# Moving the decays of the second pair of old states behind the first two additions on VectorE

## The reference, cut to what matters

```
new_state[b, head] = exp(sum of dA over the 16 tokens) * old_state[b, head]      (the decay)
                   + sum over tokens of B[token] * dt*decay*x[token]              (the addition)
y_off[token]       = C[token] . old_state * exp(cumulated dA)                      (uses the old state, undecayed)
```

## Time and profile before

| what | us |
|---|---|
| median of 3 runs (lowest, highest) | 1969.38 (1961.38, 1970.03) |
| time of the profiled execution | 1973.41 |
| its span (first to last instruction) | 1971.8 |
| TensorE busy | 1912.7 (97%) |
| VectorE busy | 1059.2 (54%) |
| ScalarE busy | 739.8 (38%) |
| GpSimd busy | 112.4 (6%) |
| mean granted clock of TensorE | 0.977 |

### The profile page before, as it was taken

One profiled execution on the slowest core, in us unless ns is written; L12 is line 12 of the kernel. 1 busy time (PEld: TensorE's weight loads), 2 busy tenths in 40 slices (PEclk: granted clock), 3 DMA queues, 4 the chain that ended last, 5 costly groups with the idle time before them and its releaser, 6 DMA issues.

```text
span 1971.8 us, 31921 instructions
## 1 busy us (share of the span) xinstructions
PE 1912.7 (97%) x12877; PEld 1858.7 (94%) x12877; DVE 1059.2 (54%) x1339; ACT 739.8 (38%) x1157; POOL 112.4 (6%) x219
## 2 busy tenths in 40 slices
PE   8999999999799999999999999998799999999998
PEld 7999999999799999989998998987799999999998
DVE  6442443345687664556567677765745433442444
ACT  5221332223477643334545445542333221221222
POOL 2000000000012100001011011100000000000000
PEclk9999999999899999999999999997899999999999
DMA  4222222222222243334224323322622222222222
GB/s 141 74 66 75 73 78 73 76 69 79 101 73 70 66 127 89 96 92 122 85 71 114 105 84 108 98 71 76 220 74 70 75 75 74 74 76 74 75 66 77
DMA packets 268066, 171.68 MB, mean 87 GB/s; under 512 B 6534, under 2 KB 259642, under 8 KB 267677
## 3 DMA queue, kind: packets, MB, share of 16 engines
q1 hardware_dynamic: 239840, 129.52, 22.8%
q0 software_dynamic: 7072, 26.34, 4.2%
q10 hardware_dynamic: 21072, 14.69, 2.4%
HBM read 150.03 MB, written 20.48 MB: 86 GB/s over the span
## 4 chain that ended last, share of the span: by engine, by line
PE 88%; DVE 6%; ACT 3%; issue 2%; DMA 1%; DVEq 0%; ACTq 0%
PE pu L633 79%; PE pn L890 2%; PE pn L830 1%; PE pn L840 1%; PE pn L858 1%; PE pn L881 1%; ACT w_hi L987 1%; PE pn L862 1%; DMA merged<-gate_spill 1%; DVE w_lo L1376 1%; PE pu L901 0%; DVE xc L1370 0%; PE pu L692 0%; PE pn L650 0%; DVE bc L1370 0%
## 5 line engine op out<-in xcount | busy, mean ns | idle before, releaser
L1376 DVE TENSOR_TENSOR w_lo<-w_raw,w_hi 128x1024 fp32r<-128x1024 f32 x240 | 295.7, 1232 | 504.0 <-ACT w_hi L987 502.0
L633 PE MATMUL pu<-act_hi,w_hi 128*128 128x320 f32 x2336 | 543.2, 314 | 19.0 <-DVE h_b L1829 9.0
L633 PE MATMUL pu<-act_lo,w_hi 128*128 128x320 f32 x2336 | 535.4, 310 | 2.0 <-DVE act_lo L1417 1.9
L633 PE MATMUL pu<-act_hi,w_lo 128*128 128x320 f32 x2336 | 535.2, 310 | 0.0
L987 ACT ACTIVATE w_hi<-w_raw 128x1024 fp32r<-128x1024 f32 x240 | 253.6, 1056 | 540.0 <-PE pu L633 536.3
L633 PEld LDWEIGHTS pu<-act_hi,w_hi 128*128 128x128 f32 x2336 | 394.0, 189 | 33.0 <-issue 26.0
L633 PEld LDWEIGHTS pu<-act_lo,w_hi 128*128 128x128 f32 x2336 | 393.0, 189 | 3.3 <-DVE act_lo L1417 3.0
L633 PEld LDWEIGHTS pu<-act_hi,w_lo 128*128 128x128 f32 x2336 | 393.3, 189 | 0.0
L633 PE MATMUL pu<-h_hi,w_hi 128*128 128x320 f32 x1056 | 241.4, 310 | 0.7 <-DVE ff_g L1434 0.7
L633 PE MATMUL pu<-h_lo,w_hi 128*128 128x320 f32 x1056 | 241.4, 309 | 0.0
L633 PE MATMUL pu<-h_hi,w_lo 128*128 128x320 f32 x1056 | 241.4, 309 | 0.0
(11 more groups left out here) (319 smaller groups left out, 2011.7 us busy)
## 6 DMA issues: line engine op xcount, KB each, us to landing
w_raw<-in_ffn_w_up_dram SPq DMA_DIRECT2D x87, 512.0 KB, 3.8
w_raw<-in_w_in_dram SPq DMA_DIRECT2D x73, 512.0 KB, 3.9
w_raw<-in_ffn_w_down_dram SPq DMA_DIRECT2D x32, 512.0 KB, 3.8
w_raw<-in_w_br_ssd_dram SPq DMA_DIRECT2D x16, 512.0 KB, 3.4
w_raw<-in_ffn_w_down_dram SPq DMA_DIRECT2D x16, 384.0 KB, 3.3
es<-e_spill POOLq DMA_DIRECT2D x40, 128.0 KB, 2.9
merged<-gate_spill POOLq DMA_DIRECT2D x8, 640.0 KB, 4.9
h_a<-in_state_ssd_h_dram POOLq DMA_DIRECT2D x8, 512.0 KB, 6.2
```

The costliest lines, as they stand in the source:

```text
L633: ins = pe.matmul(dst[:, h, :], w[:, side, c, :], a[:, k, h * HALF:(h + 1) * HALF], start=(at == 0), stop=(at == n - 1))
L1376: dve.tensor_tensor(w_lo[:, side, :, :], w_raw[:, side, :, :], w_hi[:, side, :, :].bitcast(F32), ALU.subtract).then_inc(s["w_lo_done"], 1)
```

## The change

Two lines change places, in each of the two branches. With a middle unit (groups 0 to 2), `decay_states(1)` moves from ahead of `xbc_taps` to behind `new_states(0)`, ahead of `xbc_silu`. Without one (group 3), `new_states(0)` goes ahead of `decay_states(1)`. The instructions, their number and their sizes stay as they are, and so do the programs of the other engines.

```diff
                 if middle:
                     for q in range(PAIRS):
                         add_square(SQ_GRP + g * SQG + q, q % 2, SEQ)
-                    decay_states(1)
                     xbc_taps(*middle[0][1:])
                     new_states(0)
+                    decay_states(1)
                     xbc_silu(*middle[0][1:])
                 else:
+                    new_states(0)
                     decay_states(1)
-                    new_states(0)
                     for q in range(PAIRS):
                         add_square(SQ_GRP + g * SQG + q, q % 2, SEQ)
```

## The result

The changed kernel took 1980.66 us (median of 6 runs, 1978.08 to 1985.12) beside 1969.51 for the kernel before (6 runs, 1961.38 to 1972.05): a ratio of 1.0069, with a 95% interval of 1.0047 to 1.0091. That is 9 to 18 us slower, with 13.6 us in the middle; the plain difference of the two medians is 11.15 us. Forecast were 1981.8 us and +12.4. The profiled execution took 1982.1 us with a span of 1980.5, 8.7 more than the span before; its mean clock is 0.977, as before.

What follows compares the result with a forecast made beforehand. TensorE, busy 1912.7 of 1971.8 us, was taken to bound the kernel. Delay of 9.1 us plus 3.3 us of clock gave +12.4 us on the median 1969.38: 1981.8 us (0.63% slower), range 1971.5 to 1990.

Steps and rivals of the forecast that it cites:

- The old place was free: Ahead of VectorE's weight cut: removing the decays brings the first additions no earlier, 0 us, bound 0.1 us a group.
- The new place has no cover: Behind the first pair's additions VectorE has no idle time: 2.28 us delay in each of 4 groups, 9.1 us.
- The size of the waits: TensorE's waits for the additions to the second pair of states: 18.1 us in sum in place of 9.0.
- the two terms of the forecast: Whole kernel: 9.1 us of delay plus 3.3 us for TensorE's clock, 12.4 us in all.
- The clock term: TensorE's units behind the pauses: 1.64 us each in groups 0 and 1, nothing more in 2 and 3; 3.3 us.
- rival 2: Group 3's low clock ahead of its pause falls elsewhere; 9.0 us come back, 1972.8 us (+0.2%); chance 0.13.
- Delay alone: All four groups: only the delay counts, clock about 0; +9.1 us, 1978.5 us (0.46%); chance 0.24.
- every resumption pays the full 2.65 us: TensorE's units behind all four pauses lose clock in full: +15.4 us, 1984.8 us (0.78%); chance 0.12.
- Absorption later: Later TensorE waits (weight tile, merge DMA) take up part of the delay: 1979.5 us, or 1977.2; chance 0.09.

Runs made afterwards that it cites:

- second comparison: The unaltered changed kernel measured again, on another chip's set of runs, against the kernel before: 1.0059 (1.0036 to 1.0082), +11.6 us, median 1981.84.
- fifth experiment: Changed kernel plus 16 additional matmuls on TensorE behind each group's last product, against the kernel before: 1.0048 (1.0030 to 1.0066), +9.4 us, median 1979.9.
- first four experiments: Decays moved in groups 0 to 2 only, in group 3 only; decays shortened in changed order, in old order; against the kernel before: 1.0031, 1.0018, 1.0023, 0.9997.
- groups 0 to 2 alone: Changed kernel with group 3 back in its old order, against the kernel before: 1.0031 (1.0020 to 1.0042), +6.1 us, median 1977.05.
- group 3 alone: Kernel before with the decays moved in group 3 only, against the kernel before: 1.0018 (1.0002 to 1.0035), +3.5 us, median 1974.4.
- changed order, short decays: Changed kernel with the second pair's decays done for one of 8 streams only, against the kernel before: 1.0023 (1.0011 to 1.0035), +4.5 us.
- old order, short decays: Kernel before with the second pair's decays done for one of 8 streams only, against the kernel before: 0.9997 (0.9983 to 1.0010), -0.6 us.
- changed order with early additions: Changed kernel with the second pair's additions directly behind its decays, against the kernel before: 1.0011 (0.9997 to 1.0024), +2.2 us, median 1972.07.

## Why the prediction was right

**The old place was free: shown.** The forecast of 0 gained ahead of the additions held to the hundredth for the convolution (2.74 us behind the start of ScalarE's weight half in both), and shortening the decays there by 7.5 us changed the time by -0.6 us, with an interval from -3.3 to +2.0. The weight cut came early by 0.28 us, where about 0.3 was forecast.

**The new place has no cover: shown.** TensorE restarts 6.95 us behind the second addition to the first pair in group 0 (858.71 - 851.76), where 6.96 was forecast. With the decays 1.87 us shorter at the new place most of the loss went; with the additions placed early in both orders, the decays' place was again worth 10.0 us. The 2.28 us a group stand in all four restarts. The sum of 9.1 us alone lies inside the interval of the second comparison and just below that of the first.

**The size of the waits: right, with shifts between the groups.** 18.1 us were forecast, 17.5 measured. The pauses were to be 4.05, 3.30, 4.55 and 6.23 us and were 3.70, 3.77, 3.29 and 6.78. The restart is set by VectorE, but the pause's beginning by TensorE's last products, and how long these take depends on the clock, which fell in other places than before. The forecast took them as fixed. By this and by the 1.67 us ahead of group 0, the two profiled executions differ by only 8.7 us, while the two terms of the forecast came to 9.1 + 3.45 in them. That the forecast median was 1.1 us from the measured one is in part luck: the two sets of runs of the changed kernel spread over 7 and 11 us.

**The clock term: right in the trace, an estimate in the time.** Forecast were 1.64 us each for the units behind groups 0 and 1 and nothing for groups 2 and 3, 3.3 in all; measured 1.29, 2.74, -0.30 and -0.28, 3.45 in all. The sum is nearer than its two parts, so part of the agreement is luck. The busy matmuls of the fifth experiment show that the pause is what makes these units slow. But the clock's changes elsewhere are as large: in group 3 the low stretch ahead of the pause was 12.7 us long in place of 20, and the stretch up to the restart grew by 0.05 us and not by 2.28. That is rival 2's mechanism, with 2.2 us of its 9.0. It was chance of that execution: the changed kernel's second profile, of a run of 1985.07 us, had some 20 us of low clock there.

What the clock adds on average can be estimated from the mean clock of every run. Within the runs of one kernel a lower mean clock goes with a longer time: over the 35 runs of the kernel before that stand beside the first four experiments the correlation is -0.92. A mean clock lower by 0.001 goes with 1.45 us more in the runs of the first four experiments, and with 1.22 us more in the others. By these slopes ("left" is the difference of the mean times, in us, less the clock's part):

| kernel | mean clock (before) | mean time against before | of it by the clock | left | delay by VectorE's rows |
|---|---|---|---|---|---|
| groups 0 to 2 alone | 0.9784 (0.9793) | +7.2 | 1.3 | 5.9 | 6.8 |
| group 3 alone | 0.9780 (0.9793) | +3.4 | 1.9 | 1.4 | 2.3 |
| changed order, short decays | 0.9772 (0.9793) | +4.8 | 3.2 | 1.7 | 1.6 |
| old order, short decays | 0.9793 (0.9793) | +0.1 | 0.1 | 0.0 | 0 |
| changed kernel again | 0.9760 (0.9794) | +12.4 | 4.1 | 8.3 | 9.1 |

So about 4 of the 12.4 us of the changed kernel go with the clock, beside 3.3 forecast; by the scatter of the mean clocks this is uncertain by some 1.5 us either way. It is an estimate and no separation of causes: a low clock inside a pause counts in the mean clock though it costs no time, and may be why a little less than the delay is left in three rows.

**The rivals.** Delay alone (+9.1) is inside the interval of the second comparison (7.1 to 16.1) and just outside that of the first (9.3 to 17.9); the times do not exclude it, the units behind the pauses and the mean clocks speak against it. That every resumption pays the full 2.65 us (+15.4) is inside both intervals too, so the times leave it open; in the trace it was wrong for groups 0, 2 and 3 (1.29, 1.34 and 2.36 us over the 7.06) and right for group 1 alone. The Trainium skill's rule ("TensorE: Matmul & The Clock Gate", "HAM oscillation — how this bites in real kernels") that a burst behind a pause starts throttled now agrees with all four groups; by its one half of the throttled time the unit of group 1, with a mean clock of 0.69 over 9.80 us, should lose 3.0 us, and lost 2.74. The prediction held against that rule that the pauses of groups 0 and 1 had cost nothing before; these were 1.77 and 1.02 us long, and the section is on longer waits for DMA, so they did not test it. Absorption later: 0.6 us of the shift went away behind group 3, 0.5 of it in TensorE's wait for ScalarE's copies of the last tails (3.1 us before, 2.6 after), and no more. The range began at 1971.5 us "(rival 2)", but that rival's own times are 1972.8 and 1968.5; no sum of the prediction gives the 1971.5.

## What to carry to other kernels

An engine that is busy half of the time can have its work moved for nothing or at full price, within a few microseconds: look for the wait that ends last behind the old place (here ScalarE's copy) and for idle time between the new place and whatever the bounding engine waits for (here none). Of several instructions behind a wait, put first the one that frees the bounding engine's buffer; that alone gave 7.7 us, where moving the decays lost 12 to 14. A pause of the matmul engine can cost beyond its length, in the clock of what follows, so price the pause and the unit behind it together.

## What the runs showed of the hardware

TensorE's clock fell behind a pause only some of the time. In the kernel before, the unit took 7.06 us at 1.00 after pauses of 1.02 and 1.77 us, but 8.70 us at 0.80 after one of 2.27, and there the clock fell 0.6 us behind the restart. In the changed kernel it took 8.35 to 9.80 us at 0.69 to 0.83 after pauses of 3.29 to 6.78 us. The length of the pause alone does not decide it: in the changed order with short decays a unit ran at 0.80 after 1.87 us, and in the changed order with early additions one began at 0.50 after only 0.84 us, in which the clock was low already.

The clock also fell in stretches in which TensorE shows as busy throughout. In group 3, where only the transposes and state products follow each other, it stood at 0.50 for 12.7 to some 20 us, and in group 0 of the kernel before from 849.5 to 855.5, over the state products. The same work does not always run slow: in the changed kernel's profile group 3 did it at 1.00 up to 1346.3, for some 5 us.

Executions of the changed kernel differed by 7 us (1978.08 to 1985.12), more than half of the effect under study. Most of such scatter goes with the mean clock, as the correlation of -0.92 above shows. With 12 runs of a kernel beside 35 of the other, the intervals here were still 0.22 to 0.33% wide.
